# Stick-breaking attention: the two score rows of an item are scored at two different distances ahead

## The chip, the cores and the metric

The kernel runs on one core of one Trainium2 chip. The metric is the device time of one execution in microseconds (us). Fewer is better. The trace is one profiled execution, read by engine: PE is TensorE (matmuls), PEld its weight loads, DVE is VectorE, ACT is ScalarE, POOL is GpSimd, SP is SyncE.

## The reference, cut to what matters

Two residual layers run over 1024 tokens of width 1024. Layer 0 mixes tokens with a short convolution, layer 1 with stick-breaking attention of 16 heads of 64. Only the attention stage of layer 1 is touched. For each head and each block of queries it computes:

```python
mask = key_pos[None, :] < t[:, None]
z = jnp.einsum("bhqd,bhkd->bhqk", qb, kf) * scale
log_keep = jnp.where(mask, jax.nn.log_sigmoid(-z), 0.0)
later = lax.cumsum(log_keep, axis=3, reverse=True) - log_keep
log_a = jax.nn.log_sigmoid(z) + later
a = jnp.where(mask, jnp.exp(log_a), 0.0)
return jnp.einsum("bhqk,bhkd->bhqd", a, vf)
```

The kernel writes the same as products: keep = sigmoid(-z), a running product of keep from the last key backwards, and a = sigmoid(z) times that product one key on.

## The kernel before, in words

All large products are computed as three matmuls of split operands (high times high, high times low, low times high), so every matmul operand has a "hi" part, made by ACT, and a "lo" part, made by DVE as the difference.

The stage works on pairs of heads, `hp` = 0 to 7, in the function `pair` that every engine has. A pair has 8 items `it`: head `hh = it // 4` of the pair, and within it the query block `t = it % 4` of 256 tokens. An item has two rows r = 0 and 1 of 128 queries each. Row r of block t has `key_count(r, t)` = 256 t + 128 (r + 1) keys, from 128 to 1024. The rows are numbered `hp * 16 + 2 * item + r`.

The way of one row through the engines:

- PE `z`: the scores of the row into PSUM banks 2r and 2r + 1 (the second bank only beyond 512 keys), and a masking matmul (lines 2595 to 2597).
- ACT `sigmoids`: `keep` and then `sig` out of PSUM (lines 1313, 1314).
- DVE `scan`: the running product over `keep` (line 1913).
- POOL `weigh`: `sig` times the shifted `keep` (line 968), which gives the attention weights.
- PE `turn`: transposes of the weights, chunk by chunk of 256 keys, both rows of the item together, into bank 4 or 5 (line 2646). An item of block t has t + 1 chunks.
- ACT and DVE `chunk`: the hi part `aT_hi` (line 1339), then the lo part `aT_lo` (line 1955).
- PE `weighted`: the product with the values into bank 6 (lines 2662, 2663), and at the item's end ACT `o_low` (line 1370) and DVE `o_sum` (line 2016), which POOL stores with a DMA (line 985).

The order of each engine's instructions is written out by hand in `pair`. In step `it` each engine first deals with both rows of item it + 1 (z, sigmoids, scan, weigh) and with the chunks of item `it`. Between them PE has projection work for the next pair of heads, in steps of three 512-column matmuls (`fill`; lines 2334 to 2336). `FILL` says how many steps go to each place: after the first two turns (two numbers) and ahead of each later `weighted`. Six pieces of 8 steps make a pair's projection; piece p lies in bank `PIECE_BANK[p]` = 3, 7, 1, 3, 7, 1, and DVE copies each out into `tf` when it is done (`finished`, lines 1612 and 1929). Before a row is scored into bank 1 or 3, PE waits for that copy (`evacuated`). At the ends of items 1 and 2 and inside items 4 and 5, ACT and DVE turn `tf` into the operands of the next pair (`project`, `lo_part`; lines 1325 and 1942).

The last pair (`last`) has nothing to project; it fills with steps of the output projection over the memory attention (`memory_steps`, counts in `FILL_LAST`), of which items 0 and 1 have none.

Buffers: `keep` and `sig` are indexed by item parity and row. Row 0 of item it + 2 goes to the buffer that row 0 of item `it` is transposed from.

Of the kernel before, what the change touches and what calls it, by code (L numbers as in the profile page):

```python
# [108 lines left out]
def trunk(nc, xT, memT, wpack, vectors, out):  # L109

    base = {}
# [24 lines left out]
    with ExitStack() as ctx:  # L136
# [435 lines left out]

        CHUNKS_BEFORE = [sum(j % 4 + 1 for j in range(it)) for it in range(9)]
# [267 lines left out]
        def _(pool):  # L841
# [44 lines left out]
            for i in range(LAYERS):  # L886
# [66 lines left out]
                if i % 2 == 1:  # L953
# [17 lines left out]
                    def pair(hp, last):  # L971
                        for it in range(ITEMS):
# [73 lines left out]
        def _(act):  # L1046
# [100 lines left out]
            for i in range(LAYERS):  # L1147
# [160 lines left out]
                else:  # L1308
# [75 lines left out]
                    for piece in (6, 7):  # L1384
                        project(0, 0, piece, piece)
                    act.wait_ge(me_stored, 16 * MHEADS * (i + 1))
# [190 lines left out]
        def _(dve):  # L1577
# [107 lines left out]
            for i in range(LAYERS):  # L1685
# [221 lines left out]
                else:  # L1907
# [51 lines left out]
                    def pair(hp, par, last, first=False):  # L1959
                        for it in range(ITEMS):  # L1960
# [15 lines left out]
                            if last and it == ITEMS - 1:  # L1976
                                for c in range(min(t + 1, 2)):
                                    chunk(hp, it, c)
                                for r in range(2):
                                    finished(r)  # L1980
                            if not (last and it == ITEMS - 1):
                                for r in range(2):
                                    row = hp * ROWS + (2 * (it + 1) + r)
                                    scan(row, (it + 1) % 2, r, (it + 1) % 4)
                                    if r == 0:
                                        for c in range(min(t + 1, 2)):
                                            chunk(hp, it, c)
                                    finished(r)
# [44 lines left out]
                    for n in range(2):  # L2033
                        values(0, 0, n, 6 + n)
                    dve.wait_ge(me_stored, 16 * MHEADS * (i + 1))
# [295 lines left out]
        def _(pe):  # L2331
# [94 lines left out]
            for i in range(LAYERS):  # L2426
# [156 lines left out]
                else:  # L2583
# [107 lines left out]
                    def pair(hp, par, last, first=False):  # L2691
# [14 lines left out]
                        for it in range(ITEMS):  # L2706
                            t = it % 4
                            if it == ITEMS - 1 and first:
                                pe.wait_ge(zeros_made, 3)
                            if it == ITEMS - 1 and not last:  # L2710
                                pe.wait_ge(sqk_lo_ready, hp * 8 + 16)
                                pe.wait_ge(sqk_hi_ready, hp * 12 + 24)
                            counts = FILL_LAST[it] if last else FILL[it]
                            if last and it == 5:
                                pe.wait_ge(evacuated, base["E", i][2] + 6)
                            for r in range(2):
                                if not last and (it, r) in ((1, 1), (5, 0), (5, 1)):
# [216 lines left out]
```

## Time and profile before

| | |
|---|---|
| median of 3 runs | 2651.57 us |
| lowest and highest | 2646.75 and 2653.51 us |
| profiled execution, first to last instruction | 2646.9 us |
| PE busy in it | 2562.6 us (97%) |
| PEld busy | 2130.7 us (80%) |
| DVE busy | 1784.0 us (67%) |
| ACT busy | 1204.7 us (46%) |
| POOL busy | 719.9 us (27%) |
| first `sigmoids` to last `weigh` start | 1333.0 to 1873.5 us |

The page gives no separate time for what lies around the span of the profiled execution; the span alone is 4.7 us under the median of the runs. A matmul's busy time in these rows is longer than the time from its start to the next one's, because matmuls overlap: a step of three 512-column matmuls shows three times 0.39 us and takes 0.69 us from start to start. A lost time on PE is therefore read from start to start.

### The profile page before, as it was taken

To read this page: it belongs to the slowest core of one execution; us is meant where nothing else is said; L and a number is where in the kernel's file an instruction comes from. 1 tells how busy PE (TensorE), PEld (TensorE's weight loads), DVE (VectorE), ACT (ScalarE), POOL (GpSimd) and SP (SyncE) were. 2 spreads that over 40 slices of the span, in tenths; PEclk is the share of its full clock that TensorE was granted. 3 is DMA by queue.
4 is the path that set the end of the run, shared out by engine and by line. 5 is a ranking of instruction groups with operands and counts; after the bars stand their busy time and mean duration, and the time that the engine had idled before them with its cause. 6 is when DMAs were issued, how large, how long until landed. Compare 5 with 4: busy or idle time off the path is not lost.

```text
span 2646.9 us, 34791 instructions
## 1 busy us (share of the span) xinstructions
PE 2562.6 (97%) x12320; PEld 2130.7 (80%) x12320; DVE 1784.0 (67%) x2247; ACT 1204.7 (46%) x2027; POOL 719.9 (27%) x523
## 2 busy tenths in 40 slices
PE   8899999999999999999999999998899999999999
PEld 8688887888888887887878888886788888887887
DVE  6566666167756577775677777777648665758667
ACT  6463333144434443335666666665424443444332
POOL 2502220102323222233033333333120322222322
PEclk9899999999999999999999999999999999999999
DMA  6412225213433456534111111112321342437634
GB/s 208 152 40 72 78 90 191 80 63 116 146 116 119 151 177 246 217 147 159 49 37 33 33 32 32 32 32 107 125 101 53 139 161 77 152 133 273 236 145 157
DMA packets 85923, 311.39 MB, mean 118 GB/s; under 512 B 10417, under 2 KB 10417, under 8 KB 73137
## 3 DMA queue, kind: packets, MB, share of 16 engines
q1 hardware_dynamic: 74304, 261.17, 28.0%
q0 software_dynamic: 11216, 42.47, 4.5%
q10 hardware_dynamic: 288, 6.29, 0.6%
q8 instruction: 64, 1.05, 0.2%
q14 instruction: 51, 0.41, 0.0%
HBM read 220.24 MB, written 89.65 MB: 117 GB/s over the span
## 4 chain that ended last, share of the span: by engine, by line
PE 79%; DVE 7%; issue 7%; ACT 4%; POOL 1%; DMA 1%; SPq 0%; ACTq 0%; DVEq 0%; POOLq 0%
PE ps L2334 25%; PE ps L2336 24%; PE ps L2335 24%; PE ps L2646 1%; POOL sig L968 1%; DVE aT_lo L1955 1%; PE ps L2662 1%; DVE tile_lo L2203 1%; DVE w_lo L1584 1%; DVE keep L1913 1%; ACT keep L1313 1%; PE ps L2663 1%; PE ps L2595 1%; ACT sq L1325 1%; PE ps L2596 1%
## 5 line engine op out<-in xcount | busy, mean ns | idle before, releaser
L2334 PE MATMUL ps<-tile_hi,g_hi 128*128 128x512 f32 x1680 | 661.3, 394 | 7.7 <-DVE tile_lo L2203 5.2
L2336 PE MATMUL ps<-tile_hi,g_lo 128*128 128x512 f32 x1680 | 658.3, 392 | 0.0
L2335 PE MATMUL ps<-tile_lo,g_hi 128*128 128x512 f32 x1680 | 654.7, 390 | 0.0
L2334 PE MATMUL ps<-xg_hi,w_hi 128*128 128x512 f32 x1024 | 412.6, 403 | 4.5 <-DVE xg_lo L1783 3.3
L2336 PE MATMUL ps<-xg_hi,w_lo 128*128 128x512 f32 x1024 | 402.6, 393 | 0.0
L2335 PE MATMUL ps<-xg_lo,w_hi 128*128 128x512 f32 x1024 | 402.1, 393 | 0.0
L2334 PEld LDWEIGHTS ps<-tile_hi,g_hi 128*128 128x128 f32 x1680 | 316.2, 188 | 76.1 <-issue 5.5
L2336 PEld LDWEIGHTS ps<-tile_hi,g_lo 128*128 128x128 f32 x1680 | 316.0, 188 | 71.5
L2335 PEld LDWEIGHTS ps<-tile_lo,g_hi 128*128 128x128 f32 x1680 | 316.3, 188 | 69.0
L1482 ACT ACTIVATE g_hi<-quads 128x512 fp32r<-128x512 f32 x310 | 194.9, 629 | 359.0 <-PE ps L2336 328.8
L2132 DVE TENSOR_TENSOR g_lo<-quads,g_hi 128x512 fp32r<-128x512 f32 x310 | 281.4, 908 | 107.1 <-ACT g_hi L1482 103.1
L1016 POOL TENSOR_TENSOR tsum<-quads 128x1024 f32<-128x1024 f32 x62 | 152.9, 2465 | 367.9 <-DVE g_lo L2132 209.5
L1023 POOL TENSOR_TENSOR quads<-quads 128x512 f32<-128x512 f32 x62 | 85.4, 1377 | 542.4 <-DVE g_lo L2132 542.4
L2334 PEld LDWEIGHTS ps<-xg_hi,w_hi 128*128 128x128 f32 x1024 | 194.3, 190 | 42.1 <-issue 6.8
L2336 PEld LDWEIGHTS ps<-xg_hi,w_lo 128*128 128x128 f32 x1024 | 193.9, 189 | 42.3
L2335 PEld LDWEIGHTS ps<-xg_lo,w_hi 128*128 128x128 f32 x1024 | 194.5, 190 | 35.9 <-issue 0.7
L968 POOL TENSOR_TENSOR sig<-sig,keep 128x127 f32<-128x127 f32 (+7 forms) x128 | 161.4, 1262 | 196.5 <-DVE keep L1913 196.1
L1584 DVE TENSOR_TENSOR w_lo<-raw,w_hi 128x1024 fp32r<-128x1024 f32 x88 | 115.5, 1315 | 119.3 <-ACT w_hi L1055 118.6
L2294 DVE TENSOR_TENSOR x<-x,ps 128x512 f32<-128x512 f32 x168 | 114.6, 682 | 114.9 <-PE ps L2336 114.7
L1913 DVE TENSOR_TENSOR_SCAN keep<-keep 128x128 f32<-128x128 f32 (+7 forms) x128 | 186.2, 1456 | 5.5 <-ACT keep L1313 3.9
L1055 ACT ACTIVATE w_hi<-raw 128x1024 fp32r<-128x1024 f32 x88 | 92.9, 1056 | 151.0 <-PE ps L2336 146.7
L1482 ACT ACTIVATE g_hi<-tsum 128x512 fp32r<-128x512 f32 x124 | 78.1, 630 | 121.9 <-PE ps L2336 115.2
(277 smaller groups left out, 4338.4 us busy)
## 6 DMA issues: line engine op xcount, KB each, us to landing
quads<-wpack SPq DMA_DIRECT2D x62, 1024.0 KB, 5.9
raw<-wpack SPq DMA_DIRECT2D x88, 512.0 KB, 3.3
d_split<-x SPq DMA_DIRECT2D x116, 256.0 KB, 6.3
tile_lo<-d_tile SPq DMA_DIRECT2D x30, 512.0 KB, 7.5
d_tile<-R SPq DMA_DIRECT2D x46, 256.0 KB, 6.4
d_tile<-x SPq DMA_DIRECT2D x46, 256.0 KB, 6.1
cquads<-wpack SPq DMA_DIRECT2D x10, 1024.0 KB, 4.8
tile_hi<-d_split SPq DMA_DIRECT2D x10, 1024.0 KB, 8.5
```

Source lines behind the costliest of these rows:

```text
L968: pool.tensor_tensor(sig[:, par, r, 0:n - 1], sig[:, par, r, 0:n - 1], keep[:, par, r, 1:n], ALU.mult).then_inc(a_ready, 1)
L1016: pool.tensor_tensor(tsum[:], quads[i][p][:, 1:3, :], quads[i][p][:, 0:2, :], ALU.subtract).then_inc(t_ready, 1)
L1023: pool.tensor_tensor(quads[i][p][:, 1, :], quads[i][p][:, 3, :], quads[i][p][:, 1, :], ALU.subtract).then_inc(t_ready, 1)
L1055: act.activation(w_hi[s][:], raw[s][:], ACT.Copy).then_inc(w_hi_ready, 1)
L1482: act.activation(g_hi[i][q][:].rearrange("p (a c) -> p a c", a=1), granule_source(i, c % 2, q).rearrange("p (a c) -> p a c", a=1), ACT.Cop ...
L1584: dve.tensor_tensor(w_lo[s][:], raw[s][:], fp(w_hi[s][:]), ALU.subtract).then_inc(w_lo_ready, 1)
L1913: dve.tensor_tensor_scan(k, k, k, 1.0, ALU.mult, ALU.bypass).then_inc(scanned, 1)
L2132: dve.tensor_tensor(g_lo[i][q][:], granule_source(i, c % 2, q), fp(g_hi[i][q][:]), ALU.subtract).then_inc(g_lo_ready, 1)
L2294: dve.tensor_tensor(xs, xs, ps[:, b, :], ALU.add).then_inc(x_added, 1)
L2334: pe.matmul(out, whi, mhi, start=start, stop=False, skip_group_check=chained)
L2335: pe.matmul(out, whi, mlo, start=False, stop=False, skip_group_check=chained)
L2336: return pe.matmul(out, wlo, mhi, start=False, stop=stop, skip_group_check=chained)
```

## The change

`row_ahead(it, j)` gives the rows that step `it` deals with: (it + 1, row 1) for j = 0, and (it + 2, row 0) for j = 1. Row 1 of an item is scored at the start of the step before it, in the place that row 0 had; row 0 is scored one place earlier than that, in the middle of step it - 2. For blocks t = 0 and 1 that middle place lies on PE between the two first groups of projection steps, for t = 2 and 3 behind the last `turn` of the item. ACT, DVE and POOL follow the same order. `FILL` and `FILL_LAST` stay as they are. In item 4 of the last pair (`late`) the second row is put at the item's end. The waits for the copies of the projection pieces and for the next pair's operands move with the rows they guard. A row is scored ahead of the first pair.

```diff
+        def row_ahead(it, j):
+            return divmod(2 * (it + 1) + 1 + j, 2)
 (POOL)
-                            if not (last and it == ITEMS - 1):
-                                for r in range(2):
-                                    weigh(hp * ROWS + (2 * (it + 1) + r), (it + 1) % 2, r, (it + 1) % 4)
+                            for j in range(2):
+                                item, r = row_ahead(it, j)
+                                if not (last and item >= ITEMS):
+                                    weigh(hp * ROWS + (2 * item + r), item % 2, r, item % 4)
...
+                    weigh(2, 1, 0, 1)
 (ACT)
-                            for r in range(2):
-                                if not (last and it == ITEMS - 1):
-                                    sigmoids(hp * ROWS + (2 * (it + 1) + r), (it + 1) % 2, r, (it + 1) % 4)
-                                if r == 0:
-                                    for c in range(min(t + 1, 2)):
-                                        chunk(hp, it, c, first)
+                            late = last and it == ITEMS // 2
+                            ahead(0)
+                            for c in range(min(t + 1, 2)):
+                                chunk(hp, it, c, first)
+                            if t < 2 and not late:
+                                ahead(1)
...
                                 chunk(hp, it, c, first)
                                 if it == ITEMS - 1 and not last:
                                     project(hp + 1, 1 - par, 4 + c)
+                            if t >= 2:
+                                ahead(1)
...
                                            ).then_inc(o_low_ready, 1)
+                            if late:
+                                ahead(1)
 (DVE)
-                                for r in range(2):
-                                    row = hp * ROWS + (2 * (it + 1) + r)
-                                    scan(row, (it + 1) % 2, r, (it + 1) % 4)
-                                    if r == 0:
-                                        for c in range(min(t + 1, 2)):
-                                            chunk(hp, it, c)
-                                    finished(r)
+                                ahead(0)
+                                for c in range(min(t + 1, 2)):
+                                    chunk(hp, it, c)
+                                finished(0)
+                                if t < 2 and not late:
+                                    ahead(1)
+                                finished(1)
...
+                            if t >= 2 or late:
+                                ahead(1)
                             if t >= 1:
                                 finished(t + 1)
 (PE)
-                            for r in range(2):
-                                if not last and (it, r) in ((1, 1), (5, 0), (5, 1)):
-                                    pe.wait_ge(evacuated, hp * 6 + (v0 + 6 + (1 if it == 1 else 3 + r)))
-                                if it < ITEMS - 1:
-                                    z(hp * ROWS + (2 * (it + 1) + r), par, (it + 1) // 4, r, (it + 1) % 4,
-                                      False)
-                                elif not last:
-                                    z(hp * ROWS + (ROWS + r), 1 - par, 0, r, 0, False)
+                            def ahead(j):
+                                item, r = row_ahead(it, j)
+                                if last and item >= ITEMS:
+                                    return
+                                if not last and (item, r) in ((2, 1), (6, 0), (6, 1)):
+                                    pe.wait_ge(evacuated, hp * 6 + (v0 + 6 + (1 if item == 2 else 3 + r)))
...
+                            ahead(0)
                             for c in range(min(t + 1, 2)):
                                 turn(hp, it, c, par, first)
-                            for r in range(2):
-                                fill(counts[r])
+                            fill(counts[0])
+                            if t < 2 and not late:
+                                ahead(1)
+                            fill(counts[1])
...
                                 if c + 2 <= t:
                                     turn(hp, it, c + 2, par, first)
+                                if t >= 2 and c + 2 == t:
+                                    ahead(1)
+                            if late:
+                                ahead(1)
```

## Rows read from the trace of the kernel before

**Rows 1.** Page, head and busy time: us, share of the span, instructions

```profile
span 2646.9 us, 34791 instructions
PE 2562.6 (97%) x12320; PEld 2130.7 (80%) x12320; DVE 1784.0 (67%) x2247; ACT 1204.7 (46%) x2027; POOL 719.9 (27%) x523
```

**Rows 2.** Windows, stage and last pair: length, busy us, granted clock, DMA share, GB/s

```profile
1335.00:1885.00 550.00, 512.28 (x2925) 433.75 (x2924) 422.50 (x502) 337.82 (x602) 194.83 (x188) 0.99 0.13 41
...
1815.00:1820.00 5.00, 3.28 (x16) 2.88 (x17) 2.68 (x3) 3.35 (x6) 2.15 (x2) 0.65 0.88 346
```

**Rows 3.** Waits of PE, pairs 0 to 6 (1341 to 1807 us): us, times, longest

```profile
PE ps L2662 <- DVE aT_lo L1955: 16.6, 30, 0.9
PE ps L2646 <- POOL sig L968: 3.8, 14, 0.3
```

**Rows 4.** Timeline of PE, items 2 and 3 of one pair: start, length, instruction, [idle before]

```profile
1480.84 0.45 PE L2595 MATMUL ps<-sk,sq 128*128 128x512 f32 x1
...
1487.55 0.45 PE L2595 MATMUL ps<-sk,sq 128*128 128x512 f32 x1
...
1488.47 0.44 PE L2595 MATMUL ps<-sk,sq 128*128 128x512 f32 x1
...
1489.51 1.04 PE L2646 MATMUL ps<-ident,sig 128*128 128x128 f32 x8
1490.31 0.48 PE L2334 MATMUL ps<-xg_hi,w_hi 128*128 128x512 f32 x1
...
1493.16 0.33 PE L2662 MATMUL ps<-aT_hi,sv 128*128 128x256 f32 x1
...
1495.17 0.39 PE L2334 MATMUL ps<-xg_hi,w_hi 128*128 128x512 f32 x1
...
1496.91 0.39 PE L2662 MATMUL ps<-aT_hi,sv 128*128 128x256 f32 x1 [0.87 <-DVE aT_lo L1955]
...
1497.42 0.28 PE L2595 MATMUL ps<-sk,sq 128*128 128x128 f32 x1
...
1497.76 0.33 PE L2595 MATMUL ps<-sk,sq 128*128 128x256 f32 x1
...
1498.54 1.09 PE L2646 MATMUL ps<-ident,sig 128*128 128x128 f32 x8 [0.27 <-POOL sig L968]
...
1501.34 0.38 PE L2662 MATMUL ps<-aT_hi,sv 128*128 128x256 f32 x1 [0.33 <-DVE aT_lo L1955]
```

**Rows 5.** Timeline of ACT, items 2, 3 and 5

```profile
1488.11 1.28 ACT L1325 ACTIVATE sq<-tf 64x512 fp32r<-64x512 f32 x2
1489.41 0.92 ACT L1313 ACTIVATE keep<-ps 128x896 f32<-128x896 f32 x1
...
1491.98 1.06 ACT L1313 ACTIVATE keep<-ps 128x1024 f32<-128x1024 f32 x1
...
1518.47 2.60 ACT L1325 ACTIVATE sk<-tf 64x512 fp32r<-64x512 f32 x4
```

**Rows 6.** Timeline of DVE, items 0 to 3 and 5

```profile
1480.63 0.69 DVE L1929 SCALAR_TENSOR_TENSOR tf<-ps,R 128x512 f32<-128x512 f32 x1 [2.35 <-PE ps L2336]
...
1488.77 1.41 DVE L1942 TENSOR_TENSOR sq<-tf,sq 64x512 fp32r<-64x512 f32 x2
...
1492.31 1.26 DVE L1955 TENSOR_TENSOR aT_lo<-ps,aT_hi 128x512 fp32r<-128x512 f32 x2
...
1494.09 2.32 DVE L1913 TENSOR_TENSOR_SCAN keep<-keep 128x1024 f32<-128x1024 f32 x1
...
1520.47 2.61 DVE L1942 TENSOR_TENSOR sk_lo<-tf,sk 64x512 fp32r<-64x512 f32 x2
```

**Rows 7.** Last pair: PE's waits (1807 to 1885 us), and one DVE entry

```profile
PE ps L2334 <- DVE piece L1972: 4.0, 3, 1.6
PE ps L2646 <- POOL sig L968: 2.9, 1, 2.9
...
1830.02 4.13 DVE L1996 TENSOR_TENSOR mf_lo<-mf_lo,mf_hi 128x1024 fp32r<-128x1024 f32 x2
```

More of the change, by code:

```diff
@@ L1345, in pair @@
                             t, hh = it % 4, it // 4
-                            for r in range(2):
-                                if not (last and it == ITEMS - 1):
-                                    sigmoids(hp * ROWS + (2 * (it + 1) + r), (it + 1) % 2, r, (it + 1) % 4)
-                                if r == 0:
-                                    for c in range(min(t + 1, 2)):
-                                        chunk(hp, it, c, first)
+                            def ahead(j):
+                                item, r = row_ahead(it, j)
+                                if not (last and item >= ITEMS):
+                                    sigmoids(hp * ROWS + (2 * item + r), item % 2, r, item % 4)
+                            late = last and it == ITEMS // 2
[4 more added lines that the diff above has]
+                                ahead(1)
                             if not last and it in (0, 3, 7):
@@ L1385, in _ @@
                         project(0, 0, piece, piece)
+                    sigmoids(2, 1, 0, 1)
                     act.wait_ge(me_stored, 16 * MHEADS * (i + 1))
@@ L1980, in pair, with ahead @@
                                     finished(r)
-                            if not (last and it == ITEMS - 1):
-                                for r in range(2):
-                                    row = hp * ROWS + (2 * (it + 1) + r)
-                                    scan(row, (it + 1) % 2, r, (it + 1) % 4)
-                                    if r == 0:
-                                        for c in range(min(t + 1, 2)):
-                                            chunk(hp, it, c)
-                                    finished(r)
+                            def ahead(j):
+                                item, r = row_ahead(it, j)
+                                if not (last and item >= ITEMS):
+                                    scan(hp * ROWS + (2 * item + r), item % 2, r, item % 4)
+                            late = last and it == ITEMS // 2
+                            if not (last and it == ITEMS - 1):
+                                ahead(0)
[5 more added lines that the diff above has]
+                                finished(1)
                             if not last and it in (0, 3, 7):
@@ L2034, in _ @@
                         values(0, 0, n, 6 + n)
+                    scan(2, 1, 0, 1)
                     dve.wait_ge(me_stored, 16 * MHEADS * (i + 1))
@@ L2716, in pair, with ahead @@
-                            for r in range(2):
-                                if not last and (it, r) in ((1, 1), (5, 0), (5, 1)):
-                                    pe.wait_ge(evacuated, hp * 6 + (v0 + 6 + (1 if it == 1 else 3 + r)))
-                                if it < ITEMS - 1:
-                                    z(hp * ROWS + (2 * (it + 1) + r), par, (it + 1) // 4, r, (it + 1) % 4,
-                                      False)
-                                elif not last:
-                                    z(hp * ROWS + (ROWS + r), 1 - par, 0, r, 0, False)
+                            def ahead(j):
+                                item, r = row_ahead(it, j)
+                                if last and item >= ITEMS:
+                                    return
+                                if not last and (item, r) in ((2, 1), (6, 0), (6, 1)):
+                                    pe.wait_ge(evacuated, hp * 6 + (v0 + 6 + (1 if item == 2 else 3 + r)))
+                                if last and (item, r) == (6, 0):
+                                    pe.wait_ge(evacuated, base["E", i][2] + 6)
+                                if (item, r) == (ITEMS, 0):
+                                    if first:
+                                        pe.wait_ge(zeros_made, 3)
+                                    pe.wait_ge(sqk_lo_ready, hp * 8 + 16)
+                                    pe.wait_ge(sqk_hi_ready, hp * 12 + 24)
+                                z(hp * ROWS + (2 * item + r), par if item < ITEMS else 1 - par, item % ITEMS // 4, r, item % 4,
+                                  False)
@@ L2724, in pair @@
+                            late = last and it == ITEMS // 2
+                            counts = FILL_LAST[it] if last else FILL[it]
+                            ahead(0)
                             for c in range(min(t + 1, 2)):
                                 turn(hp, it, c, par, first)
-                            for r in range(2):
-                                fill(counts[r])
+                            fill(counts[0])
+                            if t < 2 and not late:
+                                ahead(1)
```

8 lines of the change are left out of this document (1 added, 7 removed).

## The prediction, made before the changed kernel was built or run

> **What bounds the kernel now.** First the page: PE is busy for 97% of the span [rows 1]. Then the windows: over the 550 us of the attention stage PE is busy 512 us, DVE 422, ACT 338, POOL 195, at a granted clock of 0.99 [rows 2]. So the stage is bound by PE's work, and the change neither adds nor removes a matmul. It can only move the gaps between PE's instructions. Third, PE's waits over the seven pairs that project: 16.6 us for the low parts of the transposed weights and 3.8 us for `weigh` [rows 3]. Idle time understates a stall, so fourth I took the timeline of PE and measured from start to start.
>
> The seven pairs repeat, so one pair is enough. In item 2 the last three projection matmuls start at 1495.17; at 0.71 us a step (four steps from 1490.31 to 1493.16) the last `weighted` could start at 1495.88 and starts at 1496.91: 1.03 us lost [rows 4]. It waits for a low part that DVE makes behind the scan of 1024 keys, which starts at 1494.09 and takes 2.32 us [rows 6]. The scores of item 4 take about 0.35 us a row (1497.42 to 1497.76, so 1498.11), yet the next transposes start at 1498.54: 0.43 us lost, for `weigh` of those 1024 keys. Then two steps, and the first `weighted` of item 3 at 1501.34, where 1498.54 + 0.80 + 1.43 = 1500.77 was due: 0.57 us lost [rows 4]. Items 6 and 7 repeat the first two of these (14 waits for `weigh` in 7 pairs [rows 3]). With smaller losses of about 0.3 at the third chunk of item 3, 0.5 at that of item 7 and 0.1 at item 6's transposes (my estimates, from what is left of the 30 waits of rows 3), a pair loses 2 x (1.03 + 0.43) + 0.57 + 0.9 = 4.4 us, seven pairs 31 us. That is all the change can take from them.
>
> **What goes.** In item 2 no scan stands any more between chunks 0 and 1 and chunk 2 on DVE: row 1 of item 3 comes first, and the next scan, 128 keys, comes behind the last chunk. The 1.03 us go, twice a pair. The last row's `weigh` starts behind a scan that begins some 3 us after the item's start instead of 1494.09 - 1487.55 = 6.5 us after it, so the 0.43 (twice) and the 0.1 go too. The extra row of scores behind the last transposes covers the 0.3 and 0.5. Removed: 3.8 us a pair; item 3's 0.57 is dealt with below.
>
> **What comes: the first chunk of an item.** FILL is unchanged, and the scan ahead of chunk 0 is now row 1 (1024 keys in item 2) instead of row 0 (896). PE covered the old scan with row 1's own scores; that cover is gone. Item 2, T = 1487.55:
> - PE: scores of row 1, 1489.51 - 1488.47 = 1.04; transposes 0.80; four steps 2.85. PE is at the first `weighted` at T + 4.69. Before it came there at T + 5.61, without a stall [rows 4].
> - ACT: behind the operands of the next pair (`sq`, from 1488.11 for 1.28) `keep` can't start before T + 1.86 (1489.41), and takes 1.06 for 1024 keys: T + 2.92 [rows 5].
> - DVE: scan 2.32 and the first of two low parts (half of 1.26) end at T + 5.87 [rows 6]. Queued behind this scan on DVE are both low parts and the copy of a projection piece; PE waits for the first of them.
> Stall: 5.87 - 4.69 = 1.2 us. Bounds: 0.6 if ACT's operand work were over when the scores are there, 1.8 if DVE's is late as well (below). I take 1.2, since rows 5 show ACT late in every pair's item 2. Item 6 has four operand casts (2.60 us, rows 5) instead of two; they now run behind the sigmoids of the row scored in the middle of item 5, and end near the item's end. They hold `o_low` and then `keep` to about T + 2.0. Stall 1.3.
>
> Item 3, T' = 1497.42: PE needs 0.35 + 0.80 + 2 x 0.71 = 2.6 us to the first `weighted`. ACT starts the first sigmoid at about T' + 2.0, as in item 2 (0.3 after the item's start come `o_low` and two casts). Before, the first low part was there at 1501.34 - 0.05, so T' + 3.87. The row is now 256 keys instead of 128. The step from one size to the next is (1.06 - 0.92) = 0.14 us for a sigmoid, but there are two ahead of the high part, so 0.3 later: T' + 4.2. Stall 1.5 to 1.6 in place of 0.57 (in the old order PE had the other row's 0.35 as cover). Item 7 has five steps there and no stall.
>
> **What comes: the projection pieces.** Row 1 of items 2 and 6 needs bank 3, in which a piece has just ended. DVE's copy runs from 1480.63 to 1481.32, and PE reaches item 1's scores at 1480.84 [rows 4, 6]. Before, row 0 of item 2 (0.75 us) came first and hid it. Now PE waits 0.5 us, and the same in item 5: 1.0 a pair. DVE is free for the copy, since the scan in front of it (640 keys) is hidden by four steps. If it weren't, the cost would be up to 0.7 more at each.
>
> **What comes: the shared port.** `weigh` of row 0 of item 3 now runs at the very start of item 2, beside DVE's `sq` differences, which must end before the scan. Such a pair of differences takes 1.41 us at 1488.77, and 2.61 us at 1520.47 with a `weigh` beside it [rows 6]. DVE would end it at about T + 3.8 in place of T + 2.6, and the scan was due at T + 2.9. Bounds 0 and 0.9 in items 2 and 6; I take 0.3 each, because the overlap is partial.
> The Trainium skill ("SBUF — State Buffer", "Who interferes with whom") has the pair of ports between VectorE and GpSimd as an exclusive lock against a GpSimd operation that reads SBUF, when the VectorE operation has two SBUF inputs: the later one waits for the whole of the other. The 2.61 against 1.41 agrees in direction. By that rule the differences would start only when `weigh` ends, and the cost would be the upper bound; by the rows I stay in the middle.
>
> **Sum.** A pair: -3.8 - 0.57 + 1.2 + 1.3 + 1.55 + 1.0 + 0.6 = +1.3. The port's part is the one I trust least; without it the sum is +0.7. I take +1.0, seven pairs +7 us. Rows moved from one item into another change nothing else: the matmuls are the same ones. On POOL the store of an item's sum keeps its place behind two `weigh`s; POOL is busy 195 of 550 us [rows 2], the next item but one waits for the store, and I cost it at nothing (if POOL were late there, DVE's `o_sum` and so `weighted` of the next item would be). SP's queue isn't touched.
>
> **The last pair.** Its first items have no fill. There the old order waits 2.9 us for `weigh` [rows 7], and the clock is granted at 0.65 in 1815 to 1820 [rows 2], after PE had idled. Row 1's scan is now ready sooner, but `weigh` still stands behind the same DMA issues on POOL, so I give that wait -1. In item 2 two differences of 4.13 us stood behind a scan of up to 2.9 us and in front of chunk 2, and PE waited for both; now the scan isn't there: -2.5. The clock may come back a little sooner: -0.5. Against that, PE waits 4.0 us for copies of pieces in items 5 and 6 [rows 7]. Those copies stand on DVE behind a scan. In item 5 the scan of 896 keys (keep 0.92 and about 2.0) now starts just ahead of the piece's end: +1.4. In item 6 row 1 of 1024 keys is in front, and PE comes to the wait one row earlier: +1.4. With 0.2 for the rest, the pair comes to -1.
>
> Total: +7 - 1 = +6 us, so 2646.9 + 6 = 2652.9 for an execution like the profiled one. The page shows nothing around the span; the median of the runs is 4.7 us above it, and against the median the forecast is 2651.6 + 6 = 2657.6. About 0.3% (8 us) is what a measurement of this kernel tells from no change, so the forecast lies inside "same" by a little.
>
> **The rivals.**
> - *A, the port is a full lock.* The cost is the upper bound, 0.9 in place of 0.3, in items 2 and 6, and the waits for the pieces grow by 0.3: 7 x 1.5 = 10 more, 2668. For it: 2.61 against 1.41. Against: other pairs of the two engines' operations, such as the low parts at 1492.31, show no stretch. Chance 0.20.
> - *B, faster: the deadline of the first chunk is met.* If ACT is not held by the casts and chunk 0's low part is ready when PE comes, the stalls of 1.2, 1.3 and 1.55 don't come, and each pair gains 4.4 - 1.0 = 3.4: 7 x 3.4 + 1 = 25 us, 2627. It decides at T + 4.69 in item 2. For it: the sigmoids and scan of only one row come at once, and the large rows start half an item sooner. Against: even with ACT free the chain 1.04 + 0.3 + 1.06 + 2.32 + 0.63 is 5.35. Chance 0.14, with the cases in which only a part of them stays away.
> - *C, the last pair gives more.* If its clock doesn't fall and the piece waits grow by half of what I say, it gives -6: 2652. Chance 0.16.
> - *D, nothing happens,* because stalls only change places: inside C's range.
>
> **How the numbers follow.** Forecast 0.50 with its own range 2650 to 2663, of which 0.18 lies beyond +8 us and 0.32 within; A 0.20, of which 0.19 slower; C and D 0.16, all same; B 0.14, faster. Slower 0.37, same 0.49, faster 0.14. The range 2642 to 2668 leaves B's core and A's end out, about 2 in 10.
>
> **What would show it.** In the changed trace the wait of 0.87 at the third chunk of items 2 and 6 and the 0.27 for `weigh` are gone. In their place `weighted` waits for the low part of chunk 0 over 1 us in items 2, 3 and 6, and scores wait 0.3 us or more for the `tf` copy twice a pair. If PE's waits for low parts in pairs 0 to 6 fall well under 16.6 us, the forecast is wrong and B right. If `sq` differences take over 2.4 us in item 2, A is right. In the last pair the wait for `mf_lo` shrinks and those for pieces grow.

## The result, and the profile after

| | before | after |
|---|---|---|
| median of 5 runs | 2651.57 us | 2672.14 us |
| lowest and highest | 2646.75 and 2654.97 us | 2671.74 and 2672.61 us |
| ratio of the times | | 1.0077, 95% interval 1.0065 to 1.0088 |
| span of the profiled execution | 2646.9 us | 2670.1 us |

The change makes the kernel 20.6 us slower. The forecast was +6, the range ended at 2668: right direction, far too small, and 4 us outside the range.

The page of the changed kernel has PE, DVE, ACT and POOL as busy as before [rows 1]; the span alone grew.

```profile
span 2670.1 us, 34791 instructions
PE 2561.7 (96%) x12320; PEld 2135.8 (80%) x12320; DVE 1788.8 (67%) x2247; ACT 1204.0 (45%) x2027; POOL 719.1 (27%) x523
```

To place the growth I took the starts of all 64 `o_low` on ACT's timelines, one for each item. The last `o_low` of pair 6 and of pair 7 start at 1808.04 and 1888.88 us before and at 1824.31 and 1912.46 after. So the last pair grew from 80.84 to 88.15, that is 7.3 us. Each of pairs 1 to 6 grew from 66.8 to 68.7, by 1.85 to 1.97; with pair 0 it is +14 for seven pairs. About 2 us were there ahead of the stage, whose first `o_low` starts at 1347.89 and 1350.70 (0.8 of that is the extra row). Kernels with the old order begin it anywhere from 1347.9 to 1350.3 as well, so those 2 us are the profiled execution's own.

Within a pair the gaps between the `o_low` of neighbouring items changed by -0.43, +0.83, 0, +0.3, +0.88, +1.37, -1.06 and 0 us (items 0 to 7, means of pairs 1 to 6).

PE's waits over pairs 0 to 6 of the changed kernel (1341 to 1824 us; total, times, longest), against [rows 3]. The 16.6 us for low parts became 31.2, the 3.8 us for `sig` are gone, and waits for copies of pieces are new:

```profile
PE ps L2688 <- DVE aT_lo L1971: 31.2, 21, 1.6
PE ps L2621 <- DVE tf L1628: 3.6, 7, 0.5
PE ps L2621 <- DVE tf L1945: 3.1, 7, 0.5
```

One mid pair on PE's timeline: item 1's scores, the transposes of item 2 (T = 1494.71), and the first `weighted` of items 2, 3 and 6, against [rows 4]:

```profile
1487.78 0.49 PE L2621 MATMUL ps<-sk,sq 128*128 128x512 f32 x1 [0.46 <-DVE tf L1945]
...
1495.74 1.04 PE L2672 MATMUL ps<-ident,sig 128*128 128x128 f32 x8
...
1501.08 0.38 PE L2688 MATMUL ps<-aT_hi,sv 128*128 128x256 f32 x1 [1.55 <-DVE aT_lo L1971]
...
1508.76 0.38 PE L2688 MATMUL ps<-aT_hi,sv 128*128 128x256 f32 x1 [1.40 <-DVE aT_lo L1971]
...
1535.63 0.38 PE L2688 MATMUL ps<-aT_hi,sv 128*128 128x256 f32 x1 [1.55 <-DVE aT_lo L1971]
```

The other engines at item 2, against [rows 5, 6]. On ACT the casts stand ahead of `keep`:

```profile
1495.27 1.27 ACT L1330 ACTIVATE sq<-tf 64x512 fp32r<-64x512 f32 x2
1496.56 1.03 ACT L1318 ACTIVATE keep<-ps 128x1024 f32<-128x1024 f32 x1
```

On DVE the two differences take 2.13 in place of 1.41, then come the scan and the low parts; item 6's differences take 2.84:

```profile
1495.92 2.13 DVE L1958 TENSOR_TENSOR sq<-tf,sq 64x512 fp32r<-64x512 f32 x2
1498.08 2.29 DVE L1929 TENSOR_TENSOR_SCAN keep<-keep 128x1024 f32<-128x1024 f32 x1
1500.29 1.26 DVE L1971 TENSOR_TENSOR aT_lo<-ps,aT_hi 128x512 fp32r<-128x512 f32 x2
...
1529.41 2.84 DVE L1958 TENSOR_TENSOR sk_lo<-tf,sk 64x512 fp32r<-64x512 f32 x2
```

POOL has its `weigh` of 896 keys beside both:

```profile
1495.02 1.77 POOL L972 TENSOR_TENSOR sig<-sig,keep 128x895 f32<-128x895 f32 x1 [1.96 <-DVE keep L1929]
...
1529.57 2.14 POOL L972 TENSOR_TENSOR sig<-sig,keep 128x895 f32<-128x895 f32 x1 [1.96 <-DVE keep L1929]
```

The last pair of the changed kernel, PE's waits from 1824 to 1910 us, against [rows 7]:

```profile
PE ps L2688 <- DVE aT_lo L1971: 8.7, 3, 4.8
PE ps L2360 <- DVE piece L1988: 8.0, 3, 4.1
PE ps L2672 <- POOL sig L972: 1.2, 1, 1.2
```

Its items 0 to 4 changed by +0.2 us together, item 5 by +4.6 and item 6 by +2.5. On DVE's timeline in item 5 three scans stand ahead of the copy of a piece, two of them stretched (768 keys take 1.75 us and 896 take 2.02 us where POOL does nothing beside them):

```profile
1874.22 1.49 DVE L1929 TENSOR_TENSOR_SCAN keep<-keep 128x640 f32<-128x640 f32 x1 [1.84 <-ACT keep L1318]
...
1876.19 2.54 DVE L1929 TENSOR_TENSOR_SCAN keep<-keep 128x768 f32<-128x768 f32 x1
...
1879.70 2.53 DVE L1929 TENSOR_TENSOR_SCAN keep<-keep 128x896 f32<-128x896 f32 x1
1882.15 0.66 DVE L1988 COPY piece<-ps 128x512 f32<-128x512 f32 x1
```

and PE waits for that copy, and again in item 6:

```profile
1882.87 0.50 PE L2360 MATMUL ps<-mf_hi,w_hi 128*128 128x512 f32 x1 [4.12 <-DVE piece L1988]
...
1893.32 0.47 PE L2360 MATMUL ps<-mf_hi,w_hi 128*128 128x512 f32 x1 [3.05 <-DVE piece L1988]
```

Behind each wait PE's granted clock is 0.66 of full over 5 us (a mean of its two levels, 2.4 and 1.2 GHz). Windows of the changed kernel: length, busy us by engine, clock, DMA share, GB/s:

```profile
1883.00:1888.00 5.00, 5.00 (x21) 4.29 (x22) 2.58 (x2) 0.38 (x1) 1.09 (x1) 0.66 0.28 97
...
1893.00:1898.00 5.00, 4.68 (x17) 3.99 (x18) 0.17 (x1) 0.00 (x0) 0.47 (x1) 0.66 0.01 3
```

In the kernel before, the same two waits were 1.59 and 1.63 us, and this window lies behind the first of them, at full clock:

```profile
1863.00:1868.00 5.00, 5.00 (x31) 4.47 (x32) 3.03 (x3) 1.95 (x3) 0.91 (x1) 1.00 0.32 105
```

### The profile page after: what moved, and what is told of

It is laid out like the page before. It is cut to its first block, busy times and chain, and to the rows that moved or that the text cites. A ratio compares the mean times of both kernels' runs of the same rounds, so it can differ in the third digit from the quotient of the medians.

```text
span 2670.1 us, 34791 instructions
## 1 busy us (share of the span) xinstructions
PE 2561.7 (96%) x12320; PEld 2135.8 (80%) x12320; DVE 1788.8 (67%) x2247; ACT 1204.0 (45%) x2027; POOL 719.1 (27%) x523
## 4 chain that ended last, share of the span: by engine, by line
PE 82%; DVE 8%; issue 5%; ACT 2%; DMA 2%; SPq 1%; POOL 1%; DVEq 0%; ACTq 0%; POOLq 0%
PE ps L2360 25%; PE ps L2362 24%; PE ps L2361 24%; DVE keep L1929 2%; PE ps L2672 1%; PE ps L2688 1%; PE ps L2689 1%; PE ps L2621 1%; PE ps L2622 1%; DMA tile_lo<-d_tile 1%; DVE aT_lo L1971 1%; DVE w_lo L1600 1%; DVE tile_lo L2229 1%; PE ps L2491 1%; POOL R L871 0%
## 5 line engine op out<-in xcount | busy, mean ns | idle before, releaser
L2361 PEld LDWEIGHTS ps<-tile_lo,g_hi 128*128 128x128 f32 x1680 | 315.8, 188 | 68.7
L1929 DVE TENSOR_TENSOR_SCAN keep<-keep 128x128 f32<-128x128 f32 (+7 forms) x128 | 178.9, 1398 | 39.6 <-ACT keep L1318 38.4
```

Source lines behind the costliest of these rows:

```text
L1929: dve.tensor_tensor_scan(k, k, k, 1.0, ALU.mult, ALU.bypass).then_inc(scanned, 1)
L2361: pe.matmul(out, whi, mlo, start=False, stop=False, skip_group_check=chained)
```

## The experiments

All are timed beside runs of the kernel before on the same chip. "A pair" is the mean of pairs 1 to 6, read from the `o_low` starts.

| kernel | median, us | ratio to before, 95% interval | a pair, against after | last pair, against after |
|---|---|---|---|---|
| after | 2672.14 | 1.0077 [1.0065, 1.0088] | 68.7 | 88.15 |
| last_old | 2665.26 | 1.0051 [1.0037, 1.0064] | 0 | -7.1 |
| mid_old | 2657.38 | 1.0020 [1.0010, 1.0030] | -1.9 | -0.1 |
| last5 | 2666.90 | 1.0055 [1.0041, 1.0069] | 0 | -4.6 |
| hold | 2664.48 | 1.0056 [1.0042, 1.0069] | -0.8 | -0.7 |
| fill | 2655.36 | 1.0018 [1.0008, 1.0027] | -2.3 | -0.5 |
| cast | 2661.99 | 1.0041 [1.0028, 1.0054] | -1.7 | +1.3 |
| swap | 2683.21 | 1.0114 [1.0099, 1.0130] | 0 to +3.2 | +1.5 |
| best1 | 2651.26 | 1.0000 [0.9991, 1.0009] | -1.9 | -7.1 |
| best2 | 2647.95 | 0.9985 [0.9976, 0.9994] | -2.5 | -5.4 |
| best3 | 2651.47 | 0.9999 [0.9990, 1.0008] | -2.1 | -6.9 |
| old_cast | 2682.79 | 1.0115 [1.0100, 1.0131] | +2.6 | -5.3 |
| old_fill | 2651.02 | 0.9996 [0.9987, 1.0005] | -1.9 | -4.4 |

**Where the loss sits: `last_old` and `mid_old`.** All four engines get a switch that puts row 0 of an item back where it was scored before, beside row 1 (the item `it` whose second row waits for the next step):

```diff
+        PUT_OFF = {False: (), True: (0, 1, 2, 3, 4, 5, 6, 7)}    # last_old; mid_old has the two swapped
+        def put_off(last, it):
+            return it in PUT_OFF[last] if it >= 0 else ITEMS - 1 in PUT_OFF[False]
...
+                            if put_off(last, it - 1):
+                                ahead(1, it - 1)
...
-                            if t < 2 and not late:
+                            if t < 2 and not late and not put_off(last, it):
                                 ahead(1)
```

> The last pair scores its rows in the old order, pairs 0 to 6 in the new one. Theory (the loss has two parts that add: stalls before the first weighted product and before the scores in items 1, 2, 3, 5, 6 of each of seven pairs, 1.9 us a pair, and the last pair's waits for the copies of pieces, some 7 us): the last pair loses its part, so about 7 us less than the changed kernel, near 2664, and its waits for piece copies are back at 4.0 us in all. Rival (the last pair is only late because the pairs before it are, and everything comes from one source such as the shared port): no more than 2 us less, 2670 or above.

> Pairs 0 to 6 score in the old order, the last pair in the new one. Theory: seven times 1.9 us go, 13 us less than the changed kernel, near 2659, and the last pair still waits about 8 us for the copies of pieces. Rival (one source): the time is back at that of the kernel before, 2652, or stays at 2672.

The last pair in the old order gives back 7.1 us in the trace and 6.9 in the medians; the seven pairs in the old order give back 13.7 in the trace (pair 6 ends at 1810.57 instead of 1824.31) and 14.8 in the medians. The two halves add up to 21.6 in the medians, the change to 20.6.

The column of the last pair has up to 3 us in it that come from no edit. Its items 0 to 4 take 47.6 to 50.5 us in the seven traces in which this pair has the old order (50.5 in `old_fill`, where nothing in the pair was edited; the granted clock over these items is 0.83 there and 0.89 in the kernel before), and 47.1 to 48.4 in the seven with the new one. Items 5 and 6 are steady: together they take 22.8 us in each of the seven of the old order, 29.9 to 30.8 in the six of the new, and 25.4 in `last5`. So the last pair's loss is shown in items 5 and 6 alone.

**Which row does it in the last pair: `last5`.** Only row 0 of item 7 goes back (896 keys, the third of the three scans).

```diff
+        PUT_OFF = {False: (), True: (5,)}
```

> The changed kernel, but in the last pair row 0 of item 7 is scored where it was before, at the start of item 6, instead of between the fill groups of item 5. Theory: on DVE the copy of the piece no longer stands behind the 896-key scan, so item 5's wait of 4.12 us is 1.6 again; in item 6 the wait of 3.05 falls to about 1.6, since two rows of scores come before it again. 4 to 7 us less than the changed kernel with what the clock gives back, 2665 to 2668. Rival (the wait is PE's own latency or the clock): no change.

It gives back 4.6 of the 7.1: item 5 by 2.0, item 6 by 2.5. The longest of PE's waits for a piece falls from 4.1 to 2.7, not to the expected 1.6; on DVE row 0 of item 6 still stands in front. PE's waits from 1826 to 1906 in this kernel:

```profile
PE ps L2379 <- DVE piece L2001: 5.1, 3, 2.7
```

**The tf waits: `swap`.** In items 1 and 5 PE does its transposes ahead of the scores that wait for the copy, so that the copy has 0.8 us of cover.

```diff
-                            ahead(0)
+                            turned = not last and it in (1, 5)
+                            if not turned:
+                                ahead(0)
                             for c in range(min(t + 1, 2)):
                                 turn(hp, it, c, par, first)
+                            if turned:
+                                ahead(0)
```

> The changed kernel, but in items 1 and 5 of pairs 0 to 6 PE does the transposes of the item before the scores that wait for the copy of the projection piece. Theory: the transposes (0.70 us) cover the waits of 0.46 and 0.54 us for the copy, which with the restart are 0.6 and 0.7 start to start: 7 x 1.3 = 9 us less, near 2663. Rival (the copy's wait only absorbs time that would be lost at the next chunk, so taking it away moves the stall to the first weighted product of items 2 and 6): under 2 us less, and those two stalls grow from 1.55 to about 2.1 us.

A miss in the sign; the rival had the mechanism. The waits for `tf` go, and items 1 and 5 gain 0.7 each; but items 2 and 6 lose 0.75 each, since the scores reach ACT later, the two scans of item 1 now follow each other with a `weigh` beside the second, and the `weighted` that was late is later: its wait grows from 1.55 to 2.30. PE's timeline at item 2:

```profile
1505.61 0.38 PE L2688 MATMUL ps<-aT_hi,sv 128*128 128x256 f32 x1 [2.30 <-DVE aT_lo L1971]
```

So far nothing is lost or won. Most of the 11 us goes with the clock: in 5 of the 14 items 2 and 6 the loss is 2.3 in place of 0.75 us. Over the 6 us from such a wait of 2.30 us the granted clock is 0.72 in one pair and 1.00 in another (windows of `swap`):

```profile
1783.00:1789.00 6.00, 5.14 (x25) 4.79 (x26) 2.81 (x6) 0.94 (x3) 2.40 (x2) 0.72 0.00 0
1505.00:1511.00 6.00, 5.39 (x38) 5.04 (x39) 3.50 (x7) 2.37 (x6) 2.51 (x3) 1.00 0.00 0
```

Waits of 1.6 us in the changed kernel never did that in pairs 1 to 6, whose lengths agree within 0.3 us.

**The port: `hold`.** POOL holds the `weigh` of 896 keys back until DVE has scanned the row behind it.

```diff
+                                if not last and it in (1, 5) and j == 1:
+                                    pool.wait_ge(scanned, hp * ROWS + (2 * item + 2))
```

> The changed kernel, but in items 1 and 5 of pairs 0 to 6 POOL holds the product of the 896-key row back until DVE has scanned the next row, so it doesn't run beside DVE's operand differences. Nothing is left out. Theory (the product beside the differences stretches them from 1.41 to 2.13 us in item 2 and to 2.84 in item 6, and so the next scan starts 0.45 and 0.39 us after its sigmoid is ready): the differences take 1.4 us again, the stalls before the first weighted product of items 2 and 6 fall from 1.55 by about 0.4 each, 7 x 0.8 = 5 to 6 us less, near 2666. Rival (the stretch is in the records only, or the time is ACT's): the stalls stay at 1.55, 2672.

DVE's timeline at item 2 has the differences at 1.40 again, and the scan 0.45 earlier:

```profile
1495.92 1.40 DVE L1960 TENSOR_TENSOR sq<-tf,sq 64x512 fp32r<-64x512 f32 x2
1497.63 2.29 DVE L1931 TENSOR_TENSOR_SCAN keep<-keep 128x1024 f32<-128x1024 f32 x1 [0.30 <-ACT keep L1320]
```

The stall of item 2 falls by 0.47 and that of item 6 by 0.36, item 3's doesn't: 0.8 us a pair is what the overlap cost. The scan is now released by ACT's `keep`, so ACT bounds what more could be had.

**The cover: `fill`.** One projection step more ahead of the first `weighted` of items 2 and 6, two more in item 3, taken from the later places of the same items.

```diff
-        FILL = [(4, 4), (2, 2, 1), (3, 1, 1, 1), (0, 2, 1, 1, 1), (4, 4), (2, 2, 1), (3, 1, 1, 1), (1, 4, 0, 0, 0)]
+        FILL = [(4, 4), (2, 2, 1), (4, 1, 1, 0), (2, 2, 1, 0, 0), (4, 4), (2, 2, 1), (4, 1, 1, 0), (1, 4, 0, 0, 0)]
```

> The changed kernel with the projection steps moved ahead of the first weighted product: items 2 and 6 have 5 steps there instead of 4, item 3 has 4 instead of 2, the later places have fewer. Theory (what the change took away is PE's cover in front of the first chunk; the later chunks have cover to spare): the stalls of 1.70, 1.55 and 1.69 us become about 1.0, 0.2 and 1.0, 2.8 us a pair, 19 us less, near 2653. Rival (the later chunks are as short of cover, and the stall only moves on): 5 us less or nothing, and waits for the low part appear at the third chunks of items 2, 3 and 6.

It gives 2.3 us a pair, most of what was expected. What is left on PE's timeline:

```profile
1499.07 0.38 PE L2688 MATMUL ps<-aT_hi,sv 128*128 128x256 f32 x1 [0.88 <-DVE aT_lo L1971]
...
1509.42 0.39 PE L2688 MATMUL ps<-aT_hi,sv 128*128 128x256 f32 x1 [0.26 <-DVE aT_lo L1971]
```

**ACT's lateness: `cast`.** The operand casts and differences at the ends of items 1 and 2 go behind the first two chunks of items 2 and 3.

```diff
-                            if not last and it in (1, 2):
-                                project(hp + 1, 1 - par, it - 1)
...
-                            if not last and it in (4, 5):
+                            if not last and it in (2, 3, 4, 5):
                                 project(hp + 1, 1 - par, it - 2)
```

> The changed kernel, but the operands of the next pair that ACT and DVE make at the ends of items 1 and 2 are made behind the first two chunks of items 2 and 3. Theory (in items 2 and 3 ACT's two casts and DVE's two differences stand in front of the row that everyone waits for): the sigmoid starts about 0.6 us sooner in item 2 and 1.3 in item 3, the scan in item 2 no longer waits for the differences; the stalls of 1.70 and 1.55 fall to about 0.6 and 0.3, 7 x 2.3 = 16 us less, near 2656; item 6, whose casts stay, keeps its 1.69. Rival (scan length alone sets the stall): items 2 and 3 keep over 1.2 us each, 2669 or more.

Item 2 gains 0.81 and item 3 0.87, 1.7 a pair where 2.3 was expected; item 6, whose casts stay, keeps its stall. PE's timeline, items 2, 3 and 6:

```profile
1497.66 0.38 PE L2684 MATMUL ps<-aT_hi,sv 128*128 128x256 f32 x1 [0.47 <-DVE aT_lo L1969]
...
1508.33 0.38 PE L2684 MATMUL ps<-aT_hi,sv 128*128 128x256 f32 x1 [0.34 <-DVE aT_lo L1969]
...
1531.62 0.38 PE L2684 MATMUL ps<-aT_hi,sv 128*128 128x256 f32 x1 [1.55 <-DVE aT_lo L1969]
```

**Together: `best1`.** `fill`, `hold` and `last_old` in one kernel.

> Three edits together: the projection steps moved (as in fill), POOL's product held back (as in hold), and the last pair in the old order (as in last_old). Theory (the parts add): 19 + 6 + 7 = 32 us less than the changed kernel, near 2641, under the kernel before. Rival (they cover the same stall, so the sum is less): no better than 2650.

The time is that of before and not 10 us under it, as the rival said. The single gains (16.8 + 7.7 + 6.9 in the medians) sum to 31.4, and 20.9 came. Most of the reason is in the rows: the held `weigh` pushes the next one back, and the transposes of items 3 and 7 wait for it again. Against the changed kernel, items 2 and 6 give the sum of the single gains (-1.17 and -1.06, where `fill` and `hold` alone gave -1.16 and -1.08). Item 3 gives 0.46 less than in `fill`, and item 7 loses 0.74: 1.2 us a pair, some 8 in seven, of the 10.5 missing. Another 1.2 are the last pairs of `fill` and `hold`, 0.5 and 0.7 shorter than in the changed kernel with nothing edited in them. POOL's and PE's timelines at item 3:

```profile
1498.49 1.77 POOL L978 TENSOR_TENSOR sig<-sig,keep 128x895 f32<-128x895 f32 x1 [7.08 <-DVE keep L1944]
...
1500.79 2.01 POOL L978 TENSOR_TENSOR sig<-sig,keep 128x1023 f32<-128x1023 f32 x1
```

```profile
1502.85 1.09 PE L2693 MATMUL ps<-ident,sig 128*128 128x128 f32 x8 [0.55 <-POOL sig L978]
```

**The version that beats both: `best2`, and `best3`.** `best2` is `fill`, `cast` and `last_old`; `best3` adds the hold in item 5 alone (the diff of `hold` with `it == 5`).

> The changed order in pairs 0 to 6 with the projection steps counted anew (as in `fill`) and with the operand casts and differences of items 1 and 2 moved behind the first two chunks of items 2 and 3 (as in `cast`); the last pair in the order of before. No hold on POOL. My theory (late engines behind the scores, each with its own cover): what each edit leaves over is what the next one takes. `fill` left 0.88 us at items 2 and 6 and 0.27 at item 3's third chunk; the cast move takes item 2's 0.88 and no more of item 3 than those 0.27, so 1.0 us a pair on top of `fill`: 2672.1 - 16.8 - 7.1 - 7 = 2641 if all of it comes, 2644 with part of it lost as in `best1`. Rival (stalls change places, PE's work and the chain ACT-DVE of one row set a floor that every version meets): no better than `best1`, 2650 to 2652.

> `best2` and in item 5 alone POOL holds the weigh of row 0 of item 7 (896 keys) back until row 1 of item 6 is scanned. Theory: the hold gave item 6 0.36 us a pair and gave back 0.54 as a wait for sig at the next transposes in `best1`; so this is -1 to +2 us against `best2`, 2640 to 2646. Rival (the port is the main thing left): 3 us faster than `best2`.

`best2` is 3.7 us faster than the kernel before, by an interval that excludes no change, but less than half of what I expected. Little of it comes from `cast`: a pair takes 66.23 us, in `fill` alone 66.40, in the kernel before 66.81. `fill` with `last_old` and without `cast` was not run; by their medians it would be at 2648.5 (an estimate: 2672.1 less 16.8 and 6.9), 0.5 us above `best2`. The moved differences stand ahead of the third chunk's low part, and the stall goes there. DVE's and PE's timelines, item 2:

```profile
1496.58 1.54 DVE L1969 TENSOR_TENSOR sq<-tf,sq 64x512 fp32r<-64x512 f32 x2
1498.15 0.56 DVE L1982 TENSOR_TENSOR aT_lo<-ps,aT_hi 128x384 fp32r<-128x384 f32 x1
```

```profile
1498.77 0.38 PE L2703 MATMUL ps<-aT_hi,sv 128*128 128x256 f32 x1 [0.70 <-DVE aT_lo L1982]
```

In `best3` item 6 gains 0.35 more and item 7 loses 0.75, the wait for `sig`, as expected; its median says +3.5 against `best2`, where -1 to +2 was expected.

**Are the two cures cures of the change? `old_fill` and `old_cast`.** The old order in all pairs, with the diff of `fill` or of `cast`.

> The order of before in every pair with the step counts of `fill`: a control of `fill`. Theory (each order wants its steps where its own stall is): items 2 and 6 get a step ahead of the first product, where nothing was late, and lose the one ahead of the third, where 1.03 us was: up to +0.7 us twice a pair; item 3 gains its 0.57 and loses a step ahead of chunks 2 and 3 (+0.3 to +0.7): +1 to +1.5 us a pair, 2659 to 2662. Rival (the new counts are better in any order, and what `fill` gave says nothing on the change): 2640 or below.

> The order of before in every pair, only the operand casts and differences of items 1 and 2 moved behind the first two chunks of items 2 and 3. Theory (the casts delay whatever is scored at the item's start, in either order): ACT's keep of item 2 starts up to 1.3 us sooner and with it the two scans; of the 1.03 + 0.43 us lost at item 2's third chunk and item 3's transposes about 0.7 goes, and of item 3's 0.57 about 0.5: -1.2 us a pair, 2643. Rival (only the new order is sensitive to them, since PE has no cover ahead of its first product): no change, 2651, or +0.3 us a pair, because the differences now stand between the low part of chunk 1 and the scan of 1024 keys: 2654.

`old_fill` changes nothing in the pairs that it edits: no item of pairs 1 to 6 by more than 0.08 us. Neither my sum nor the rival was right. In the old order the last low part of an item sets its end. The steps ahead of the third `weighted` of item 2 are 3 + 1 + 1 + 1 = 6 or 4 + 1 + 1 + 0 = 6, so it waits as long. In item 3 the 0.57 us lost at the first chunk [rows 4] are gone and come back at a later one (PE's timeline of `old_fill`):

```profile
1506.33 0.39 PE L2704 MATMUL ps<-aT_hi,sv 128*128 128x256 f32 x1 [0.68 <-DVE aT_lo L1982]
```

So what `fill` gave in the new order is a cure of the new order's stalls and not a better filling at large.

`old_cast` costs 4.5 us a pair (item 2 up to +3.0, item 3 up to +1.7), where the same edit gives 1.7 in the new order. I had -1.2 and the rival +0.3, so both failed. On DVE the differences now lie between the scan of 1024 keys and the third low part, and the `weigh` of that scan stretches them to more than twice their length:

```profile
1505.17 2.31 DVE L1938 TENSOR_TENSOR_SCAN keep<-keep 128x1024 f32<-128x1024 f32 x1
1507.51 3.09 DVE L1967 TENSOR_TENSOR sq<-tf,sq 64x512 fp32r<-64x512 f32 x2
1510.63 0.56 DVE L1980 TENSOR_TENSOR aT_lo<-ps,aT_hi 128x384 fp32r<-128x384 f32 x1
```

PE's wait at that low part grows from 0.87 to 3.42 us, and that is most of item 2's loss. Item 3's goes with the clock: at this wait the granted clock fell in all seven pairs. PE waits for nothing between item 3's transposes and its first `weighted`, and takes 4.26 us (1513.43 to 1517.69) where it took 2.80 before. PE's timeline and the window behind the wait:

```profile
1511.24 0.58 PE L2700 MATMUL ps<-aT_hi,sv 128*128 128x256 f32 x1 [3.42 <-DVE aT_lo L1980]
...
1513.43 1.93 PE L2684 MATMUL ps<-ident,sig 128*128 128x128 f32 x8
```

```profile
1511.00:1518.00 7.00, 6.76 (x27) 6.21 (x28) 3.35 (x7) 4.00 (x9) 1.58 (x3) 0.53 0.06 14
```

In the new order that place is free, since the next scan is the small one. This is what the change does bring: room for work behind the first chunks of an item. With the steps placed as in `fill`, that room was worth 0.2 us a pair (`best2`).

## Why the prediction was wrong

- **Removed, 4.4 us a pair: right.** The third chunk of items 2 and 6 no longer waits, and `sig` no longer holds item 3's transposes. (`old_fill` shows that item 3's 0.57 was no loss of its own in the old order; in the sum the error is small, since the old item's whole loss goes with its last chunk.)
- **The first chunk: right in mechanism and nearly in size.** With 1.03 for the scores, 0.79 for the transposes and 2.85 for four steps behind T = 1494.71, the first `weighted` of item 2 was due at 1499.38 and started at 1501.08: 1.70 lost, where 1.2 + 0.3 was said. Item 6: due 1533.94, started 1535.63, 1.69 against 1.3 + 0.3. Item 3: 1.55, as said. `fill` and `cast` confirm both sides of the race, PE's missing cover and ACT's casts. ACT's lateness in item 2 came as said: `keep` was said for T + 1.86 and started at T + 1.85.
- **The pieces: 0.62 and 0.70 us from start to start**, where 0.5 each was said.
- **The port: a full lock, as rival A had it, at half of A's price.** `hold` gives 0.47 and 0.36 (said: 0.3 each; bound: 0.9), because ACT's `keep` would have released the scan only 0.45 us sooner. The Trainium skill's rule ("SBUF — State Buffer", "Who interferes with whom": against a GpSimd operation that reads SBUF, a VectorE operation with two SBUF inputs that comes second waits for the whole of it) fits the rows: `weigh` ends at 1495.02 + 1.77 = 1496.79, two differences of 0.70 behind it end at 1498.19, and they ended at 1498.05. The sign set for A, differences over 2.4 us in item 2, did not show: they took 2.13, because `weigh` had started 0.90 us ahead of them; item 6 has 2.84. The kernel before could have settled A. Of the 2.61 us quoted, 0.70 are the first difference; `weigh` runs from 1520.62 for 1.91, so the second was due at 1522.53 + 0.70 = 1523.23, and it ended at 1523.08. A scan beside a `weigh` of that kernel shows it as well (1484.26 + 1.32 + 1.75 = 1487.33, ended 1487.19); POOL's and DVE's timelines of the kernel before:

```profile
1484.26 1.32 POOL L968 TENSOR_TENSOR sig<-sig,keep 128x639 f32<-128x639 f32 x1 [0.27 <-DVE keep L1913]
```

```profile
1485.15 2.04 DVE L1913 TENSOR_TENSOR_SCAN keep<-keep 128x768 f32<-128x768 f32 x1
```

- **The sum of a pair: the terms gave +1.3, I took +1.0, and it is +1.9.** The measured parts are 0.62 + 0.70 + 1.70 + 1.55 + 1.69 = 6.26, less 4.4. Rounding down cost 2 us over seven pairs and the undersized terms 4: +14, where +7 was said.
- **The last pair is the step that failed: "the pair comes to -1". It is +7.3.** Two errors. First, -3.5 was booked for waits that only moved. The wait for `weigh` went from 2.94 to 1.16 and that for `mf_lo` from 1.97 to 0, but the waits for low parts in items 0 to 2 grew from 1.51, 0.79 and 2.33 to 2.33, 1.58 and 4.82: in item 1 a stretched scan of 896 keys (2.52 us at 1835.58) now stands ahead of the first `mf_lo` pair (3.90 at 1838.03), where it had stood behind one (3.68 at 1820.14, scan at 1824.09), and a larger scan (1842.19) and the low part still come behind. That sums to +0.3. Which of these waits grows is not the same in every execution (items 0 to 4 vary by 3 us, see `last_old`), but no trace of the new order has these items more than 0.5 us under the kernel before, where 3.5 were booked; their median is 47.8 us in the new order and 48.0 in the old. I had removed a wait and not asked what the same DVE work would hold up next, although I had for the other seven pairs. Second, items 5 and 6: +1.4 each was said for the copies, measured +2.5 and +1.4 as waits, because in item 5 three scans and not two stand in front, with locks of 0.8 and 0.5 us in them. Behind each of the longer waits the granted clock was 0.66 over 5 us, which is 2 x 5 x 0.34 = 3.4 us of matmuls (an estimate from the two windows). 2.5 + 1.4 + 3.4 = 7.3, against 7.1 measured for the two items; `last5` and `last_old` confirm the place. The clock had been named only as a gain.
- **The rivals.** B (the deadline met) never applied: PE's waits for low parts nearly doubled, from 16.6 to 31.2. C had the last pair at -6. None had it as a loss, and the range ended where A alone did. That the time came out near A's 2668 is chance: the port cost 0.8 us a pair (`hold`), 6 of the 20.6 us, and not A's 1.5.

Left open: what makes items 0 to 4 of the last pair vary by 3 us, and why the clock fell behind some waits of 2.3 us and not behind others of the same length.

## What to carry to other kernels

- Moving work ahead does not remove a stall when the engine behind it has the same work in its queue. For the step that becomes first, list what each of the other engines must do before it, and what the waiting engine has as cover (work of its own that it can do meanwhile).
- Cover that comes ahead of an item's last consumer is one sum. Moving it earlier helps only where an earlier consumer is the late one.
- Price a stretch without filler by the whole queue of the engine that it waits for.
- Add the clock where a wait grows to the lengths behind which it fell here, 2.3 us and more.

## What the runs showed of the hardware

**The lock is whole, and it takes scans too.** A scan of 128 keys takes 0.41 us. In `best1` one that starts during a `weigh` of 1023 elements (1500.79 to 1502.80, above) takes 2.01: 1502.80 + 0.41 = 1503.21, and it ended at 1503.09. DVE's timeline:

```profile
1501.08 2.01 DVE L1944 TENSOR_TENSOR_SCAN keep<-keep 128x128 f32<-128x128 f32 x1
```

The scan of 768 keys in the changed kernel's last pair (2.54; 1.74 elsewhere in that pair) fits as well: the `weigh` beside it ends at 1877.11, plus 1.74 is 1878.85, and it ended at 1878.73. Low parts, which have one operand in PSUM, keep their 1.26 us beside a `weigh` (1500.29 in the changed kernel, `weigh` from 1500.46 to 1502.45).

POOL waits as well when it comes second: where the differences started 0.16 us ahead of it, `weigh` of 896 keys took 2.14 us (1529.57 in the changed kernel), against 1.77 where it came first (1495.02).

**The clock after a wait.** After waits of 3.05 and 4.12 us the granted clock was 0.66 over the next 5 us; after 2.65 us (`last5`) it was 0.66 as well; after 3.42 us (`old_cast`) it fell in seven of seven pairs; after 2.30 us it was 0.72 in one pair and 1.00 in another; after single waits of 1.6 us it stayed at 1.00. A wait in the middle can thus cost nothing or about 1.6 us more, and five such cases make 8 of the 11 us by which `swap` is slower.
